# Recurrence stage of a two-block model: inverses of 64x64 triangles by doubling on TensorE, against 32x32 blocks inverted by row steps on GpSimd and one join on TensorE

## The reference, cut to what matters

```
for each token t:                       # S is 64 x 64
    S = S * w[t] - (S @ kk[t]) (kk[t]*a[t])^T + v[t] kt[t]^T
    y[t] = S @ r[t]
```

## Time and profile before

| what | us |
|---|---|
| runs | 4590.22, 4593.15, 4598.21; median 4593.15 |
| span of the profiled execution, first to last instruction | 4578.4 |
| recurrence, first product of a pair's decays to the last product with w_o | 3076.4 to about 4035 |
| share of TensorE, VectorE, ScalarE, GpSimd busy in the whole span | 92, 35, 24, 22% |

### The profile page before, as it was taken

The page is one execution under the profiler, slowest core; times in us unless marked ns, Lnnn a source line. Parts: engine busy times, 40 slices in busy tenths (PEclk is TensorE's granted clock), DMA queues, the critical chain, the costliest instruction groups (busy, mean ns, idle before and its releaser), DMA issues.

```text
span 4578.4 us, 97226 instructions
## 1 busy us (share of the span) xinstructions
PE 4207.9 (92%) x42203; PEld 2684.8 (59%) x42203; DVE 1605.1 (35%) x3656; ACT 1117.5 (24%) x2416; POOL 1006.4 (22%) x800
## 2 busy tenths in 40 slices
PE   8999999989999899997999999987888888879999
PEld 7977787868886444652333334446666666534433
DVE  4333331242242321633111123045555665442223
ACT  1032111012101322622222221043433333221111
POOL 4334233424454003101111100144222222010000
PEclk9999999999999999998999999989999999989999
DMA  4253221222223113526999993262011100159999
GB/s 160 74 196 124 74 74 66 82 100 84 77 90 87 55 51 107 164 82 228 346 349 350 352 336 103 92 189 60 27 38 32 32 10 10 40 209 409 408 407 368
DMA packets 277267, 702.97 MB, mean 154 GB/s; under 512 B 27216, under 2 KB 77936, under 8 KB 276592
## 3 DMA queue, kind: packets, MB, share of 16 engines
q1 hardware_dynamic: 250592, 637.97, 38.0%
q0 software_dynamic: 26256, 58.79, 4.7%
HBM read 655.00 MB, written 38.93 MB: 152 GB/s over the span
## 4 chain that ended last, share of the span: by engine, by line
PE 39%; DMA 5%; DVE 5%; ACT 4%; issue 3%; SPq 0%; POOL 0%; DVEq 0%; ACTq 0%; POOLq 0%
PE bank L3254 9%; PE bank L2821 7%; DMA ring<-in_moe_w 4%; PE bank L3280 3%; PE bank L3264 3%; PE bank L3552 2%; PE bank L3502 2%; PE bank L3227 1%; PE bank L3288 1%; PE bank L3397 1%; PE bank L3385 1%; ACT arena L1704 1%; ACT arena L1815 1%; PE bank L3415 1%; PE bank L3534 1%
## 5 line engine op out<-in xcount | busy, mean ns | idle before, releaser
L2821 PE MATMUL bank<-ring,arena 128*128 128x512 f32 x1264 | 549.4, 594 | 0.4 <-DVE arena L2338 0.4
L2862 PE MATMUL bank<-arena 128*128 128x256 f32 x2256 | 506.0, 380 | 5.5 <-DVE arena L1893 5.5
L3254 PE MATMUL bank<-ring,arena 128*64 128x512 f32 x2048 | 473.4, 601 | 13.4 <-DMA ring<-in_moe_w 8.2
L2862 PEld LDWEIGHTS bank<-arena 128*128 128x128 f32 x2256 | 435.0, 199 | 60.6 <-issue 5.1
L2821 PEld LDWEIGHTS bank<-ring,arena 128*128 128x128 f32 x1264 | 238.8, 190 | 292.7 <-issue 289.9
L2862 PE MATMUL bank<-ring,arena 128*128 128x256 f32 x1584 | 356.3, 383 | 1.6 <-DVE arena L2202 1.6
L2862 PEld LDWEIGHTS bank<-ring,arena 128*128 128x128 f32 x1584 | 314.6, 216 | 35.9 <-DVE arena L2202 2.4
L3254 PEld LDWEIGHTS bank<-ring,arena 128*64 128x64 f32 x2048 | 140.1, 137 | 328.3 <-issue 322.7
L2862 PE MATMUL bank<-arena,ring 128*128 128x256 f32 x1280 | 283.0, 379 | 1.2 <-ACT arena L1556 0.7
L3280 PE MATMUL bank<-ring,arena 128*64 128x512 f32 x1024 | 260.6, 661 | 6.9 <-ACT arena L1725 6.9
L2862 PEld LDWEIGHTS bank<-arena,ring 128*128 128x128 f32 x1280 | 243.0, 190 | 35.9 <-issue 1.4
(11 more groups left out here) (463 smaller groups left out, 6352.9 us busy)
## 6 DMA issues: line engine op xcount, KB each, us to landing
ring<-in_moe_w SPq DMA_DIRECT2D x768, 512.0 KB, 9.0
ring<-in_w_in SPq DMA_DIRECT2D x21, 2048.0 KB, 7.6
ring<-in_ada_w SPq DMA_DIRECT2D x12, 2048.0 KB, 7.9
ring<-in_ada_w SPq DMA_DIRECT2D x24, 1024.0 KB, 5.4
ring<-in_w_up SPq DMA_DIRECT2D x8, 2048.0 KB, 8.4
ring<-in_w_down SPq DMA_DIRECT2D x8, 2048.0 KB, 8.0
ring<-in_na_w_qkv SPq DMA_DIRECT2D x6, 2048.0 KB, 7.9
ring<-in_w_in SPq DMA_DIRECT2D x8, 1024.0 KB, 6.4
```

Of the source, the lines that this page charges most:

```text
L2821: ins = mm(ps[:, 0:ncol], lhs(k), rhs(k), start=(k == 0 and first), stop=(k == nk - 1))
L2862: ins = mm(ps[:, HW * j:HW * (j + 1)], lhs[:, k, j, :] if len(lhs.shape) == 4 else lhs[:, k, P * j:P * (j + 1)], rhs[:, k, :], start=(star ...
L3254: ins = mm(ps, x_chosen[:, b, k, 0:CAP_L], w[x][:, n * W:(n + 1) * W], start=(k == 0), stop=(k == KD - 1))
```

## The change

T is no longer made by doubling from 2x2 blocks. Each 64x64 triangle is cut into its two diagonal 32x32 blocks and the off-diagonal one. `blocks_of` (TensorE) makes the products of the diagonal blocks, of the part that comes first in a direction ("lead") and last ("tail"), and of the off-diagonal ("off"), for the whole pair at once: 48 products each with a moving size of 32. VectorE masks them (`mask_lead`, `mask_tail`) and turns all 32 blocks of every 32 partitions with its 32x32 transpose, so that one partition holds a whole 32x32 block and the 128 partitions hold 96 of them. GpSimd inverts these in place (`invert_blocks`): 30 row steps j, each one product and one subtraction on j x (31 - j) elements, with a semaphore between any two. VectorE turns the result back twice (`turn_blocks`), and TensorE joins the two halves with two sets of 32-row products per group (`join`, `inverse`), ScalarE copying between them.

The order is new as well. Each pair has 12 steps, and after u ("beside_values") and after the state ("beside_states") of each step every engine has a slot of fixed work for the next pair; group 0 of the next pair is finished after step 11, groups 1 and 2 within its own steps 0 to 5. For the first pair the slots run alone (p = -1). The scan's state is kept as a 64x64 block per head and direction, made by 64x64 products, and one VectorE instruction adds, one scales both directions; the block mask is gone. GpSimd's factors for T are made in place in the loaded buffer, in five passes per direction; the key buffers are single instead of double, so SP loads each as soon as its reader is done (`load_beside`). The first half of w_o is loaded while the last pair runs, and six of its eight row blocks are multiplied in the last pair's steps 6 to 9.

```diff
+        def invert_blocks(p):
+            pool.wait_ge(sem("rw_blocks_turned"), p + 1)
+            link(G.memset(Y.rearrange("p c r -> p (c r)")[:, 0:SUB * SUB:SUB + 1], -1.0))
+            pool.wait_ge(sem("rw_bonus_ready"), p + 1)
+            for j in range(1, SUB - 1):
+                shape = [P, j, SUB - 1 - j]
+                rest = Y[:, 0:j, j + 1:SUB]
+                kept = products_kept.rearrange("p t d -> p (t d)")[:, 0:j * (SUB - 1 - j)].rearrange("p (c r) -> p c r", c=j)
+                link(G.tensor_tensor(kept, Y[:, j:j + 1, j + 1:SUB].to_broadcast(shape), Y[:, 0:j, j:j + 1].to_broadcast(shape), ALU.mult))
+                ins = G.tensor_tensor(rest, rest, kept, ALU.subtract)
+                if j < SUB - 2:
+                    link(ins)
+            ins.then_inc(sem("rw_blocks_inverted"), 1)
+        link(G.memset(kk_pad, 0.0))
+        factors(0, 0)
         for p in range(RW_PAIRS):
+            factors(p, 1)
             weigh_bonus(p)
+            invert_blocks(p)
             if p + 1 < RW_PAIRS:
-                factors(p + 1)
+                factors(p + 1, 0)
...
+            ps = two_banks(full(dve, "rw_tail", p), 2 * NT * SUB)
+            for hd in range(2):
+                rows = slice(hd * CH, (hd + 1) * CH)
+                lower = c_tri[rows, 0:1, :].to_broadcast([CH, 2 * NT, SUB])
+                ins = V.tensor_tensor(blocks[rows, 2 * NT:4 * NT], ps[rows, hd].rearrange("p (n s) -> p n s", s=SUB), lower, ALU.mult)
+            free(ins, "rw_tail", p)
+            taken(dve, "rw_tail", p)
+            if p >= 1:
+                dve.wait_ge(sem("rw_blocks_back"), p)
+            V.transpose(Y, blocks.rearrange("p s c -> p c s")).then_inc(sem("rw_blocks_turned"), 1)
+        def turn_blocks(p):
+            dve.wait_ge(sem("rw_blocks_inverted"), p + 1)
+            if p >= 1:
+                taken(dve, "rw_inv", p - 1, 2)
+            link(V.transpose(G1.rearrange("p s c -> p c s"), Y))
+            V.transpose(G2.rearrange("p s r -> p r s"), Y.rearrange("p c r -> p r c")).then_inc(sem("rw_blocks_back"), 1)
...
+            old, new = (state[:, b % 2] for b in (i, i + 1))
+            ps = two_banks(full(dve, "rw_state", p, i), CH).unsqueeze(2).to_broadcast([P, 2, 2, CH])
+            ins = V.tensor_tensor(new, ps, old, ALU.add)
+            free(ins, "rw_state", p, i)
+            taken(dve, "rw_state", p, i)
+            V.tensor_tensor(new, new, ends[:, p % 2, i].unsqueeze(3).to_broadcast([P, 2, 2, CH]), ALU.mult).then_inc(sem("rw_state_ready"), 1)
+            dve.wait_ge(sem("rw_state_ready"), state_of(p, i + 1))
...
+            elif i == 3 and goes_on:
+                mask_tail(n)
+            elif i == 4:
+                if goes_on:
+                    scale(n, "T", 1)
+                if p >= 1:
+                    read_out(p - 1, 2)
+            elif i == 5:
+                if goes_on:
+                    mask_g(n, 0)
+                if m < RW_PAIRS:
+                    unit_keys(m, 1)
+            elif i == 6:
+                if goes_on:
+                    mask_g(n, 1)
+                if m < RW_PAIRS:
+                    unit_keys(m, 2)
...
+            elif i == 10:
+                if p >= 0:
+                    weigh_values(p)
+                if goes_on:
+                    turn_blocks(n)
+            elif i == 11 and m < RW_PAIRS:
+                scale(m, "K", 0)
+                scale(m, "R", 0)
...
+        def blocks_of(p, key, lead):
+            ps = two_banks(open_(key, p), W)
...
+                            ins = mm(ps[to, hd, at * SUB:(at + 1) * SUB], l[rows], r[rows], start=True, stop=True)
+            close(ins, key, p)
...
+        def join(p, g):
+            ps = four_banks(open_("rw_x", p, g), SUB)
+            pe.wait_ge(sem("rw_blocks_back"), p + 1)
+            taken(pe, "rw_off", p)
+            for j in range(RW_TILES):
                 for hd in range(2):
+                    for c in range(2):
+                        for z in range(2):
+                            rows, k = sub(2 * c + z), RW_TILES * g + j
+                            ins = mm(ps[sub(2 * hd + j), 2 * c + z, :], aO[rows, hd, k, :], (G1, G2)[z][rows, hd * NT + k, :], start=True, stop=True)
+            close(ins, "rw_x", p, g)
...
+        def inverse(p, g):
+            ps = four_banks(open_("rw_inv", p, g), CH)
+            taken(pe, "rw_x", p, g)
+            for c in range(2):
+                for z in range(2):
+                    for b in range(4):
+                        rows = sub(b)
+                        ins = mm(ps[c * CH:(c + 1) * CH, b, sub(z)], xt[rows, c, z * CH:(z + 1) * CH],
+                                 (G2, G1)[z][rows, 2 * NT + (RW_TILES * g + c) * 2 + z, :], start=True, stop=True)
+            close(ins, "rw_inv", p, g)
...
-                products(p, g)
-                for lv in range(1, RW_LEVELS):
...
-                        turn_inverse(p, g, z, lv)
...
-                                ins = mm(ps[to, c, at:at + P], aT[z][rows, hd, j, :], T, start=True, stop=True)
...
-                    if beside:
-                        scan_u(*beside)
...
-                                ins = mm(ps[to, hd, at + lo:at + hi], invT[z][rows, j, c, :], X[rows, lo:hi], start=True, stop=True)
...
-                    if beside:
-                        scan_state(*beside)
...
+        for p in range(-1, RW_PAIRS):
+            for i in range(RW_STEPS):
+                if p >= 0:
+                    scan_u(p, i)
+                beside_values(p, i)
+                if p >= 0:
+                    scan_values(p, i)
+                    scan_states(p, i)
+                beside_states(p, i)
+            if p + 1 < RW_PAIRS:
+                inverse(p + 1, 0)
+                solved(p + 1, 0)
+        read_out(RW_PAIRS - 2)
```

More of the change, by code:

```diff
@@ new lines, in _ @@
+        act.wait_ge(sem("rw_const_landed"), 16 * 7)
+        for c in range(2):
+            for half in (1, 2):
+                A(xt[:, c, half * SUB:(half + 1) * SUB], c_tri[:, 1, :], ACT.Copy)
+        key_norms(0)
+        side(0, "sum", 0)
+        side(0, "sum_ex", 0)
+        side(0, "K", 0)
+        for p in range(-1, RW_PAIRS):
+            for i in range(RW_STEPS):
+                beside_values(p, i)
+                if p >= 0:
+                    scan(p, i)
+                beside_states(p, i)
+            if p + 1 < RW_PAIRS:
+                inverse(p + 1, 0)
+                solved(p + 1, 0)
@@ new lines, in _ @@
+        pe.wait_ge(sem("rw_const_landed"), 16 * 7)
+        side(0, "sum", 0)
+        side(0, "sum_ex", 0)
+        side(0, "K", 0)
+        for p in range(-1, RW_PAIRS):
+            for i in range(RW_STEPS):
+                if p >= 0:
+                    scan_u(p, i)
+                beside_values(p, i)
+                if p >= 0:
+                    scan_values(p, i)
+                    scan_states(p, i)
+                beside_states(p, i)
+            if p + 1 < RW_PAIRS:
+                inverse(p + 1, 0)
+                solved(p + 1, 0)
```

1169 lines of the change are left out of this document (614 added, 555 removed).

## The result

The changed kernel takes 4467.1 us (median of four runs, 4452.9 to 4473.3), the kernel before beside it 4592.7: a ratio of 0.9718, 95% interval 0.970 to 0.9735. That is 125.5 us faster where I had forecast 237, and outside my range (4275 to 4455). The profiled execution took 4468.4 us with a span of 4467.1.

A forecast was written before the change was run, and what follows sets the result against it. TensorE, busy 92% of the span, sets the time; a pair takes 78 us instead of 108.3. 3156 + 7 x 78 + 58 + 38 = 3798 against 4035, so 4593 - 237 = 4356 us, eight-in-ten range 4275 to 4455.

The forecast's parts named there:

- Instructions, 1772 a pair: TensorE's matrix instructions per head pair, counted from the code, fall from 2708 to 1772.
- The 78 us: Period of the loop over head pairs: 68 us plus 10 us of waiting for GpSimd, instead of 108.3.
- 61 us of TensorE work: TensorE busy 61 of 78 us a pair, 1772 instructions at 34.4 ns, so mostly at the 2.4 GHz clock.
- VectorE's wait of some 10 us for GpSimd once a pair: In step 10 VectorE waits for GpSimd's inversion, 44 us with contention against a window of 33.6 us.
- Waits of 8 us a pair: Per pair: 4 us for VectorE's side work in five slots, 3 and 1 us for copies over ScalarE.
- The N=32 instructions at 20 ns: TensorE's 480 32-column products on 64 or 32 rows cost 20 ns each, 9.6 us a pair.
- Start, 5 us later: Before the first scan step: blocks turned at 3103, inversion 44 us, 9 more us, scan at 3156, 5 later.
- the 10 us gap before the last steps: The scan's 10 us wait for the output weights goes, since they are loaded during the last pair.
- C: Rival: TensorE's clock falls; at 1.2 GHz half the time, period 93 us, total 4461 us; chance 0.12.
- D: Rival: VectorE becomes the bound by contention or dear transposes, period 88 us, total 4426 us; chance 0.07.
- E: Rival: GpSimd pays for every short row, inversion 135 us, period 169, total 4993 us; chance 0.05 slower, 0.02 same.
- both engines slowing each other: VectorE and GpSimd contend during the inversion: 8 us a pair charged to GpSimd, bounds 0 and 12.

The follow-up runs named there:

- experiment 2: Changed kernel plus 64 TensorE filler products a pair that nobody reads, in the waits for u and behind steps 4 to 10: 4520.5 us.
- experiment 14: Kernel before the change plus six dummy VectorE products of 192 elements ahead of every u and state operation: 4834.9 us.
- experiment 11: Changed kernel with leading diagonal and off-diagonal block products made for one tile of six from pair 1 on, 160 instructions a pair fewer: 4428.9 us.
- experiment 4: Changed kernel without GpSimd's two tensor-scalar passes in each factor product: 4457.7 us.
- experiment 16: Changed kernel with values weighed in slot 9, r/a0/a1 loads behind the blocks, GpSimd's factors in four tensor-tensor passes, pair 0's factors on VectorE: 4444.9 us.
- experiment 10: Changed kernel with VectorE's two transposes that turn the inverted blocks back cut to a 32-column stub from pair 1 on: 4435.8 us.
- experiment 1: Changed kernel with GpSimd's inversion cut to 3 of its 30 row steps: 4426.1 us.
- experiment 7: Changed kernel with pair 0's inversion run on VectorE in slot 10 instead of GpSimd: 4471.2 us.
- experiment 15: Changed kernel with 27 of 30 inversion steps, the turning back, and five of six tiles' leading and off-diagonal blocks left out (last two from pair 1): 4354.3 us.

## Why the prediction was wrong, step by step

- **Instructions, 1772 a pair: right**, exactly.
- **The sum, term by term.** The 78 us were 60 of TensorE's work (side work 39, read products 7, the twelve steps' own products 13), 4 of waiting for VectorE, 4 for ScalarE and 10 for GpSimd. The three pairs above have 62.2, 18.6, 4.9 and 0, and 6.5 of stops for nothing shown: 92.2.
- **61 us of TensorE work, "so mostly 2.4 GHz": this step failed.** I carried 34.4 ns an instruction over from a stream of larger products; at the old clock it is 46.5/1772 = 26 ns. The sum by parts, 60 us, was too dear by as much. And I took the clock as mostly kept. It fell to 0.74 in the mean, by turns between the two levels of 1.2 and 2.4 GHz (1.00 from 3465 to 3469 us, 0.50 from 3476 to 3483), and 46 became 62. Two misses of 15 us cancelled by luck, so that the busy time looks right and the mechanism isn't. The clock's 15.7 us are more than the pitch lacks against 78: without them (62.2 - 15.7 + 30) it would be 76.5. That is an estimate that no run shows, and probably too low, since with the pitch the inversion's window would shrink and part of the wait for GpSimd would come back. My own sign of being wrong, a granted clock under 0.9, is what came. Experiments 2 and 14 show that work goes with 1/clock and that idle time lowers the clock.
- **VectorE's wait of some 10 us for GpSimd once a pair: this failed too.** The inversion's size was right (40 against 44 us), its window wasn't: the same slots took 44 us instead of 33.6. In the three pairs above VectorE never waits for it, and in all seven it waits 7.8 us instead of some 70. Of the signs that I had named, GpSimd's share was 64% of the three pairs, not over 75%.
- **Waits of 8 us a pair beside it: too small.** They are 30. The 4 us for ScalarE were about right (4.9). The 4 for VectorE were 18.6, and this is the largest miss among the terms. I took VectorE's transposes at 1.27 us each, within bounds of 0.95 and 2.56: they take 1.91 to 2.07, and TensorE waits 5.5 us a pair for the two in slot 10; their removal gives 4.4. For the scalings (L2703) it waits 6.0, for u 4.8. The stops for nothing shown (6.5) were not in the sum, though the kernel before has 4.9 us a pair of them, of which the earlier trace rows show little.
- **The N=32 instructions at 20 ns: too dear by themselves** (14 ns each in the 1.80 us burst), and dearer with their stops (experiment 11: 4.9 us for 160, 31 ns each).
- **Start, 5 us later: 26 instead.** The blocks are turned at 3124.6, not 3103. GpSimd begins its factors at 3088.2, not 3081, behind a DMA for which it waits 5.4 us; they take 2.13 us for each tensor-scalar pass that I had costed like the 1.54 us row or less, and the block products with their stops stand in the way (VectorE's mask of the tail waits 6.7 us for them). Experiments 4 and 16 each take 8 us of it back. The uncovered inversion (37 us) was in my sum.
- **Tail: the 10 us gap before the last steps is gone**, as forecast. What comes behind the last output product, which I had carried over unchanged, takes 9.8 us more; 7.8 of them are VectorE's longer way behind TensorE.
- **Rivals.** C is the mechanism that came, and I had given it 0.12; its 4461 us lay outside my own range. That its pitch of 93 and its time match the 92.2 and 4467 is partly luck: it has the 10 us of waiting for GpSimd and the 60 us of work, and little of the waits above. Of D, the transposes are worth 4.4 us a pair (experiment 10), and the inversion beside VectorE at most 2.8 (experiment 1). E is refuted: steps of 30 elements in rows of one take 0.24 us, and the whole inversion 40.2, not 135.

The rule of the Trainium skill, "SBUF — State Buffer", section "Who interferes with whom", is that a VectorE instruction with two SBUF inputs contends with a GpSimd instruction that reads SBUF, and that the shared ports are an exclusive lock. The timeline of experiment 7 agrees for tensor-tensor on GpSimd (1.57 and 1.97 us for some 0.35). It differs for GpSimd's tensor-scalar: a VectorE step that began just behind it was done after 0.87 us, and the next ones were not held. I had charged 8 us a pair for both engines slowing each other in the inversion, and by the rule 12. Taking nearly all of the inversion away gave 2.8 us a pair (experiment 1), and 1.6 in the pairs where VectorE did not wait for its result.

## What to carry to other kernels

When a change takes work off the busiest engine, forecast its busy share anew and price its remaining work at both clocks; keep that case in the range with real weight, for here the gain came out at about half. Cost the new waits of every engine at the slots where the work is joined, not only the engine that got the new work. And where two errors may cancel, compare busy time and clock separately, not busy time alone.

## What the runs showed of the hardware

- Idle time alone, put beside unchanged TensorE work, raised its busy time from 93.3 to 106.1 us a pair as the granted clock went from 0.99 to 0.85 (experiment 14); 10 us less of idle time, in the changed kernel, left the clock at 0.73 (experiment 15).
- VectorE's transpose of 32x32 blocks in fp32, 128x1024: 1.91 to 2.07 us over its three lines, against an estimate of 1.27 for a product of that size by the pace of the earlier trace rows.
- GpSimd on 128x768: tensor-tensor 1.54 us, tensor-scalar 2.13. The one-input form is the dearer. The Trainium skill, "GPSIMD Engine Reference", section "4.1 Engine selection", has GpSimd about twice slower than VectorE for two inputs and at roughly line rate for one. Here it is 1.6 times slower for two inputs (VectorE 0.955), and this tensor-scalar in place takes 2.13 us, where VectorE's takes 0.75 for 1024 elements (L1976).
- TensorE took MATMUL instructions of 32 columns on 64 rows at 14 ns each, 128 in 1.80 us at a granted clock of 0.50. Around that run it stood still 3.2 and 1.5 us with nothing to wait for that the profile shows; with 160 such instructions fewer a pair, 2.2 us a pair of these stops went.
